# All feature norms of a two-block network: sums by token, root and reciprocal on 128x4, squares in the tail of the adding stages, high part first in the first two units

## What is computed

```python
def rms_norm(x, g):
    xf = x.astype(jnp.float32)
    y = xf * lax.rsqrt(jnp.mean(xf * xf, axis=-1, keepdims=True) + EPS)
    return (y * g.astype(jnp.float32)).astype(x.dtype)

x = x + merged @ w_out[i]
x = x + expert_choice_moe(rms_norm(x, g_moe[i]), w_router[i], w_exp_gate[i], w_exp_up[i], w_exp_down[i])
ple_gate = jax.nn.sigmoid(rms_norm(x, g_ple[i]) @ w_ple_gate[i])
x = x + ple_gate * (p[i] @ w_ple[i])
```

## Time and profile before

| what | value |
|---|---|
| time, median of 3 runs | 4469.36 us (4468.59 to 4471.97) |
| the profiled execution | 4467.54 us, its span 4465.8 us |
| granted PE clock, mean over the span | 0.912 of full speed |
| PE busy | 85% of the span |
| DVE, ACT, POOL busy | 40%, 28%, 3% |

### The profile page before, as it was taken

How to read it: one execution, slowest core, us unless ns; L and a number is a source line. 1 busy time by engine, 2 the same in 40 slices (tenths; PEclk the granted TensorE clock), 3 DMA queues, 4 the chain that set the end, 5 groups by cost and what they waited for, 6 DMA issues and landing times. The chain is left out here.

```text
span 4465.8 us, 46290 instructions
## 1 busy us (share of the span) xinstructions
PE 3794.0 (85%) x17300; PEld 2476.6 (55%) x17300; DVE 1780.6 (40%) x2668; ACT 1269.7 (28%) x1955; POOL 139.8 (3%) x60
## 2 busy tenths in 40 slices
PE   6769999978899979366996999988757798699997
PEld 4557877855688857224875433346523587433334
DVE  5745434177444341756334111133367443311114
ACT  3434433147343221244322000023134332100003
POOL 3500000021000000000000000000000000000000
PEclk8989999989999989667997999999867799799999
DMA  2122222110222321000223899942100121499991
GB/s 113 59 72 83 99 90 81 50 48 16 79 99 80 105 80 48 23 17 18 94 69 123 342 418 410 410 197 71 38 0 17 54 99 54 189 420 412 409 397 47
DMA packets 108849, 617.62 MB, mean 138 GB/s; under 512 B 12310, under 2 KB 12694, under 8 KB 58812
## 3 DMA queue, kind: packets, MB, share of 16 engines
q1 hardware_dynamic: 108732, 616.07, 35.6%
HBM read 612.07 MB, written 3.95 MB: 138 GB/s over the span
## 5 line engine op out<-in xcount | busy, mean ns | idle before, releaser
L325 PE MATMUL PS<-WK_r,RING_r 128*128 128x512 f32 x2096 | 832.2, 397 | 0.0
L323 PE MATMUL PS<-WK_r 128*128 128x512 f32 x1712 | 687.9, 402 | 120.5 <-DVE RING_r L320 67.9
L325 PEld LDWEIGHTS PS<-WK_r,RING_r 128*128 128x128 f32 x2096 | 404.2, 193 | 86.7
L323 PEld LDWEIGHTS PS<-WK_r 128*128 128x128 f32 x1712 | 329.7, 193 | 219.7 <-DVE RING_r L320 78.6
L324 PE MATMUL PS<-HT_r,WK_r 128*128 128x512 f32 (+1 forms) x992 | 395.5, 399 | 0.0
L1944 DVE TENSOR_TENSOR XT<-XT,PS 128x512 f32<-128x512 f32 x128 | 88.0, 687 | 579.2 <-PE PS L1870 579.2
L320 DVE TENSOR_TENSOR RING_r<-RING,WK_r 128x1024 fp32r<-128x1024 f32 x194 | 236.7, 1220 | 73.8 <-ACT WK_r L317 73.8
L325 PE MATMUL PS<-AR_r,RING_r 128*128 128x512 f32 x672 | 263.0, 391 | 0.0
L323 PE MATMUL PS<-AR_r,RING_r 128*128 128x512 f32 x640 | 251.1, 392 | 10.3 <-DVE HT_r L320 10.3
L324 PE MATMUL PS<-AR_r,WK_r 128*128 (+1 forms) x592 | 235.5, 398 | 0.0
L320 DVE TENSOR_TENSOR RING_r<-RING,RING_r 128x1280 fp32r<-128x1280 f32 (+1 forms) x80 | 115.1, 1439 | 291.7 <-ACT RING_r L317 291.7
(11 more groups left out here) (345 smaller groups left out, 5494.2 us busy)
## 6 DMA issues: line engine op xcount, KB each, us to landing
AR<-moe SPq DMA_DIRECT2D x288, 1024.0 KB, 11.1
RING<-moe SPq DMA_DIRECT2D x96, 1024.0 KB, 11.6
RING<-ff_in SPq DMA_DIRECT2D x96, 512.0 KB, 3.4
RING<-branch SPq DMA_DIRECT2D x64, 640.0 KB, 3.8
RING<-ff_out SPq DMA_DIRECT2D x48, 512.0 KB, 3.4
RING<-mix_in SPq DMA_DIRECT2D x32, 512.0 KB, 3.4
RING<-lru_in SPq DMA_DIRECT2D x20, 640.0 KB, 4.8
RING<-ple SPq DMA_DIRECT2D x16, 640.0 KB, 11.5
```

Of the source, the lines that this page charges most:

```text
L323: nc.tensor.matmul(out, r(w_high), r(x_high), start=start, stop=False)
L325: return nc.tensor.matmul(out, r(w_low), r(x_high), start=False, stop=stop)
```

## The change

`norm_pe` no longer sums with ones as the stationary operand. In `token_sums` the squares are stationary, 128 tokens at a time, and one column of ones moves: 4 float32 matmuls of one column for each of 8 pieces, 32 in all, which leave the sums by token on the partitions, 128x4. ACT takes the root of mean plus EPS of these straight from PSUM, DVE the reciprocal of 128x4. To spread the result over the partitions again, DVE multiplies it into an identity matrix (four diagonals, 128x512), and PE multiplies that by ones into bank 6 (`spread`), from where the normed pieces are made.

With `early=True` (the six norms behind an `out_stage`) the squares and the sums are made in the tail of the `out_stage`, before the barrier. `norm_dve` now writes all 8 normed pieces, then the low part of weight unit 1, then all low parts of the pieces. `first_units` takes units 0 and 1 with the high parts of x first and the low parts of x last; it serves the two feed-forward stages, NSA, both mix stages and both embeddings. LRU keeps its order on PE.

```diff
+    def token_sums(b, k, square):
+
+        for t in range(TT):
+            mm = nc.tensor.matmul(bank(b, t, 1), square[:, t * P:(t + 1) * P], cst("ones", 0, 1),
+                                  start=(k == 0 and t == 0), stop=(k == KD - 1), skip_group_check=True)
+        return mm
...
+    def norm_act(act, s, while_summed=None, early=False):
+        if not early:
+            for k in range(KD):
+                nc.scalar.activation(wk(k), XT[:, k], ACT.Square).then_inc(s["squared"], 1)
         if while_summed:
             while_summed()
-        act.wait_ge(s["mean"], 1)
-        nc.scalar.activation(wk(9), wk(8), ACT.Sqrt).then_inc(s["deviation"], 1)
-
-    def norm_pe(pe, s):
+        if not early:
+            act.wait_ge(s["summed"], 1)
+        nc.scalar.activation(STD, bank(0 if early else 7, 0, TT), ACT.Sqrt, bias=cst("eps"), scale=1.0 / D
+                             ).then_inc(s["deviation"], 1)
+
+    def norm_pe(pe, s, early=False):
+        if not early:
+            for k in range(KD):
+                pe.wait_ge(s["squared"], k + 1)
+                mm = token_sums(7, k, wk(k))
+            mm.then_inc(s["summed"], 1)
+        pe.wait_ge(s["diagonal"], 1)
+        nc.tensor.matmul(bank(6), cst("ones"), wk(8), start=True, stop=True).then_inc(s["spread"], 1)
+
+    def norm_dve(dve, s, gain, at=0, out=HT, highs=None, lows=None, first=None, second=None):
+
+        dve.wait_ge(s["deviation"], 1)
+        nc.vector.reciprocal(INV, STD).then_inc(s["inverse"], 1)
+        dve.wait_ge(s["inverse"], 1)
+        nc.vector.tensor_tensor(wk(8).rearrange("p (t c) -> p t c", t=TT), cst("ident").unsqueeze(1).to_broadcast([P, TT, P]),
+                                INV.unsqueeze(2).to_broadcast([P, TT, P]), ALU.mult).then_inc(s["diagonal"], 1)
+        if first:
+            first()
+        dve.wait_ge(s["spread"], 1)
         for k in range(KD):
-            pe.wait_ge(s["squared"], k + 1)
-            mm = nc.tensor.matmul(bank(7), cst("ones"), wk(k), start=(k == 0), stop=(k == KD - 1))
-        mm.then_inc(s["summed"], 1)
-
-    def norm_dve(dve, s, gain, at=0, out=HT, highs=None, lows=None, while_root=None):
-
-        dve.wait_ge(s["summed"], 1)
-        nc.vector.tensor_scalar(wk(8), bank(7), 1.0 / D, EPS, ALU.mult, ALU.add).then_inc(s["mean"], 1)
-        if while_root:
-            while_root()
-        dve.wait_ge(s["deviation"], 1)
-        nc.vector.reciprocal(wk(9), wk(9)).then_inc(s["inverse"], 1)
-        dve.wait_ge(s["inverse"], 1)
-        for k in range(KD):
-            nc.vector.scalar_tensor_tensor(out=out[:, k], in0=XT[:, k], scalar=par(gain, at + k), in1=wk(9),
+            nc.vector.scalar_tensor_tensor(out=out[:, k], in0=XT[:, k], scalar=par(gain, at + k), in1=bank(6),
                                            op0=ALU.mult, op1=ALU.mult).then_inc(s["normed"], 1)
-            if highs and k:
-                dve.wait_ge(s["x_high"], k)
-                low_part(lows[k - 1], HT[:, k - 1], highs[k - 1]).then_inc(s["x_low"], 1)
+        if second:
+            second()
         if highs:
-            dve.wait_ge(s["x_high"], KD)
-            low_part(lows[KD - 1], HT[:, KD - 1], highs[KD - 1]).then_inc(s["x_low"], 1)
+            for k in range(KD):
+                dve.wait_ge(s["x_high"], k + 1)
+                low_part(lows[k], HT[:, k], highs[k]).then_inc(s["x_low"], 1)
 
+    def first_units(pe, s, w, high, banks, highs, lows):
+
+        for u in range(2):
+            pe.wait_ge(s["w_split"], u + 1)
+            for k in range(KD):
+                if u == 0:
+                    pe.wait_ge(s["x_high"], k + 1)
+                at = slice(k * P, (k + 1) * P)
+                nc.tensor.matmul(bank(banks[u]), r(high[u][:, at]), r(highs[k]), start=(k == 0), stop=False)
+                nc.tensor.matmul(bank(banks[u]), r(slot(w, u)[:, at]), r(highs[k]), start=False, stop=False)
+        done = []
+        for u in range(2):
+            for k in range(KD):
+                if u == 0:
+                    pe.wait_ge(s["x_low"], k + 1)
+                at = slice(k * P, (k + 1) * P)
+                mm = nc.tensor.matmul(bank(banks[u]), r(high[u][:, at]), r(lows[k]), start=False, stop=(k == KD - 1))
+            done.append(mm)
+        return done
...
                 unit_loop(pe, unit)
+                for m in range(KD):
+                    pe.wait_ge(s["squared"], m + 1)
+                    mm = token_sums(0, m, SQ[m])
+                mm.then_inc(s["summed"], 1)
...
+                for m in range(KD):
+                    act.wait_ge(s["added"], m + 1)
+                    nc.scalar.activation(SQ[m], XT[:, m], ACT.Square).then_inc(s["squared"], 1)
...
-                norm_pe(pe, s)
-                with pe.Fori(0, FF_N // 2) as i:
+                norm_pe(pe, s, early=True)
+
+                def pair(i, j):
+                    n = i * 2 + j
+                    pe.wait_ge(s["w_split"], 2 * n + 1)
+                    pe.wait_ge(s["b_free"], n + 1)
+                    in_unit(w, 2 * j, j, WH, list(zip(XH, XL))).then_inc(s["used"], 1)
+                    pe.wait_ge(s["w_split"], 2 * n + 2)
+                    in_unit(w, 2 * j + 1, 2 + j, WH, list(zip(XH, XL))).then_inc(s["used"], 1)
...
+                for mm in first_units(pe, s, w, WH, (0, 2), XH, XL):
+                    mm.then_inc(s["used"], 1)
+                pair(0, 1)
+                with pe.Fori(1, FF_N // 2) as i:
                     for j in range(2):
-                        n = i * 2 + j
-                        pe.wait_ge(s["w_split"], 2 * n + 1)
-                        pe.wait_ge(s["b_free"], n + 1)
-                        in_unit(w, 2 * j, j, WH, list(zip(XH, XL)), 0,
-                                None if j else lambda k: pe.wait_ge(s["x_low"], k + 1)).then_inc(s["used"], 1)
-                        pe.wait_ge(s["w_split"], 2 * n + 2)
-                        in_unit(w, 2 * j + 1, 2 + j, WH, list(zip(XH, XL))).then_inc(s["used"], 1)
+                        pair(i, j)
...
                 norm_pe(pe, s)
-                with pe.Fori(0, KD // 4) as i:
-                    for j in range(4):
-                        n = i * 4 + j
+                first_units(pe, s, w, WH, (0, 1), XH, XL)
+                pe.wait_ge(s["p_low"], 2)
+                for n in range(KD):
+                    j = n % 4
+                    if n >= 2:
                         pe.wait_ge(s["w_split"], n + 1)
                         pe.wait_ge(s["free"], n + 1)
-                        in_unit(w, j, j, WH, list(zip(XH, XL)), 0,
-                                None if j else lambda k: pe.wait_ge(s["x_low"], k + 1))
-                        pe.wait_ge(s["p_low"], 2)
-                        in_unit(w, j, 4 + j, WH, list(zip(PH, PL)), KD).then_inc(s["gates_in"], 1)
+                        in_unit(w, j, j, WH, list(zip(XH, XL)))
+                    in_unit(w, j, 4 + j, WH, list(zip(PH, PL)), KD).then_inc(s["gates_in"], 1)
 
             @block.scalar
             def _(act):
@@ -2005,8 +2070,8 @@
...
-                mm = nc.tensor.matmul(bank(b)[0:4], par("rel_bias", 0, 4)[0:BUCKETS], HOT[:, b], start=True, stop=True)
+                mm = nc.tensor.matmul(bank(1 + b)[0:4], par("rel_bias", 0, 4)[0:BUCKETS], HOT[:, b], start=True, stop=True)
             mm.then_inc(s["rows"], 1)
-            norm_pe(pe, s)
+            norm_pe(pe, s, early=True)
             pe.wait_ge(s["shifted"], 16)
             pe.wait_ge(s["copied"], 1)
             for n in range(8):
-                if n >= 7:
-                    pe.wait_ge(s["out_copied"], n - 6)
-                nc.tensor.matmul(bank(n % 7, 0, HALF), cst("flip"), ar(7, 7)[:, n * HALF:(n + 1) * HALF],
+                if n >= 6:
+                    pe.wait_ge(s["out_copied"], n - 5)
+                nc.tensor.matmul(bank(n % 6, 0, HALF), cst("flip"), ar(7, 7)[:, n * HALF:(n + 1) * HALF],
                                  start=True, stop=True).then_inc(s["flipped"], 1)
 
         @block.scalar
         def _(act):
-            norm_act(act, s)
```

More of the change, by code:

```diff
@@ L77, in const_tables @@
         "ones": np.ones((P, P)),
+        "eps": np.full((P, 1), EPS),
         "ones64": (p // 64 == np.arange(P)[None, :] // 64).astype(float),
@@ L263, in arrived @@
         pe.wait_ge(filled[w.first + j], w.before[j] + 16 * (i + 1))
-    NORM = " squared summed mean deviation inverse normed"
+    NORM = " squared summed deviation inverse diagonal spread normed"
     SPLIT = " x_high x_low w_high w_split"
+    STD, INV = SM[:, 456:460], SM[:, 460:464]
     def split_act(act, s, highs):
@@ L375, in out_stage @@
         XH = [wk(4 + b) for b in range(2)]
-        with stage("used highs lows banked added") as (block, s):
+        SQ = [wk(8 + m) for m in range(KD)]
+        with stage("used highs lows banked added squared summed") as (block, s):
             @block.sync
@@ L817, in _, with unit @@
         def _(pe):
-            norm_pe(pe, s)
-            with pe.Fori(0, 4) as i:
```

(31 more changed lines are left out.)

39 lines of the change are left out of this document (20 added, 19 removed).

## The result

The changed kernel takes 4497.61 us (median of 4 runs, 4495.89 to 4503.85) against 4470.66 us of before (4 runs on the same chip): ratio 1.0062, 95% interval 1.0045 to 1.0080. It is slower by 27 us. The prediction was 4490, from 4472 to 4504. The profiled execution took 4496.11 us with a span of 4494.3, 28.5 more than before.

The account below looks back on a forecast made before the run. PE, busy 85% of the span, was taken to bound the kernel, with each norm a gap in its work. The stage terms sum to +20.9 us, 4490.3 on the median of 4469.36; 8-in-10 range 4472 to 4504.

Parts of the forecast that it names:

- the clock stays up: Rival: weight loads count as work, so the new sums run at full clock; 4431 us, faster by 0.8%; chance 0.08.
- it falls late: Rival: the clock falls 5.9 us after the last wide matmul everywhere; 4473 us; chance 0.13 with all milder mixtures.
- the order costs: Rival: under high-first order PE waits longer for unit 2 everywhere, taking back 10 us; 4500 us; chance 0.14.
- The record's price and the clock: Each norm's 64 one-column records: 0.106 us each at full clock, 0.211 at half; 6.8 or 13.5 us, plus 0.3.
- When it falls: During the norm's sums, PE's clock falls to half 4.1 us after the last wide matmul; ends 2.4 and 5.9.
- The tail: Root, reciprocal, diagonals and spread, from the sums' end to the first normed piece: 3.4 us, gaining 1.7, 1.4 and 2.0.
- The LRU: Its late norm's sums start at half clock and never rise: 13.8 us for 9.81, +4.0 - 1.4 = +2.6.
- T: The start of a norm's first normed piece; in the first feed-forward before the change 342.05, 13.27 us behind the last add.
- Routers: Early norms with no weight split but the table load: 13.8 us from last add against 12.9, +1.0 each.
- Embeddings: Longer norm sums +2.4 each, unit 2 starting earlier by the high-first order -2.7 each; together -0.6.
- Between the blocks: Early norm: barrier 8.8 us later behind the last add, bias table's stage 2.6 shorter; net +6.2, between +2 and +8.
- The order: High parts first: unit 2 starts 1.6 us earlier in NSA and mixes, 2.7 in embeddings, 0.2 later in feed-forwards; LRU 0.

Follow-up runs that it names:

- 128 columns: The changed kernel, but each of the 32 sum matmuls moves 128 columns of ones instead of one: 4441.17 us, ratio 0.9935.
- order alone: The kernel before with only the high-part-first order, its norm unchanged: 4465.33 us, ratio 0.9996.
- norm alone: The changed kernel with the old order of normed pieces, low pieces and units: 4505.97 us, ratio 1.0084.
- rounded kernels: The changed kernel with 128 columns of ones, squares and ones in the rounded format: 4419.59 us; the same with the order of before: 4428.06 us.

## Why the prediction was right

The theory was that the sums by token cost more than those that they replace because the clock falls during records of one column. Its rivals were that the clock stays up, that it falls late, and that the order costs. By its steps:

**The record's price and the clock: right.** 0.106 and 0.211 were read from other matmuls; the sums gave 0.112 from start to start and, where PE ran at half clock throughout (the first mix), 13.81 for 64 records (13.5 and the 0.3 of hand-over forecast). The LRU's take the same 13.81 at the same 0.213, though the profile's clock reads 1.00 there, so at the start of the span it is the spacing of the records that tells. The 0.106 was a small misreading: 54 is a window's count, and the gate's records too start 0.112 apart, so 64 at full clock are 7.2 and not 6.8 (7.30 with 128 columns). The kernel with 128 columns turned the loss of 27 us into a gain of 26 by its medians, 29 by its ratio, where the rival of the clock that stays up had 38. That rival had the price of a full clock roughly right; with one column the clock fell. The Trainium skill, "TensorE: Matmul & The Clock Gate", section "HAM oscillation", asks for no long idle gaps; the windows above have none between 328 and 332, and the clock fell there. For records of one column the trace does not bear that rule out.

**When it falls: too late by a little.** I took 4.1 us after the last wide matmul. In the first feed-forward it was 2.3 (327.52 to 329.84), in the ten norms that start at full clock 2.3 to 4.9, 3.6 in the mean; the scatter is as wide as the error. The early norms' sums took 9.2 to 11.6, 10.4 in the mean, where 9.7 was forecast with 0.3 of hand-over; all twelve together 140.9, where the prediction's terms add to 134.6 with their hand-overs. The earlier fall and the price of 0.112 are each about half of it. The milder rival, a late fall, went the wrong way.

**The tail: right.** 3.37 for 3.4; spread 2.08 for 2.1, diagonals 0.69.

**The shifts by stage**, read as after less before at the last adds and first squares, in us:

| stage | forecast | measured |
|---|---|---|
| LRU | +2.6 | -0.3 |
| feed-forwards | +0.5, +1.8 | +1.4, +2.2 |
| NSA | 0.0 | +0.6 |
| between the blocks | +6.2 | +5.0 |
| mixes | +1.5, +2.5 | +0.9, +7.0 |
| routers with experts | +1.0, +1.0 | +3.1, +1.9 |
| embeddings | -0.3, -0.3 | +1.2, +1.2 |
| final norm | +4.4 | +4.4 |

They add to +28.6 where +20.9 was forecast, inside the range but a third more, and the mis-sized terms are these. *The sums* fell short by some 6. *The LRU*: its T came 2.6 later (35.02), as forecast, and its last add did not; two executions of that same code end the block 5 us apart, so -0.3 says nothing against the term. *The second mix*: its norm gave +4.2 (forecast +4.1); what follows its T lasted 748.4 here, and 744.2 to 746.4 in the seven experiments with the same order, so about 3 of its +7.0 belong to this execution. It is luck that these 3 and the LRU's -2.9 cancel in the sum. *Routers*: the first one's sums took 10.94, and T came 15.0 behind the last add for 13.8; behind T the two stages were 1.0 and 1.5 longer than before, which the forecast had at nothing and whose cause stays open. *Embeddings*: the norms cost 3.2 each for 2.4, and the order gave 2.0 back instead of 2.7.

**Between the blocks: the sum right, the reading of it incomplete.** +8.8 for the late barrier and -2.6 for a shorter stage were measured as +8.8 and -3.9. But the term is not the price of being early: with one column, late costs as much. It is the price of long sums in either place. With 128 columns it turns into one, of 4.1 us.

**The order: direction right, size open.** PE's waits ahead of unit 2 came as forecast: NSA 1.08 (1.3), feed-forward 2.90 (3), unit 2 at T + 15.4 (15.6) and T + 18.0 (17.4):

```profile
361.74 0.50 PE L339 MATMUL PS<-WK_r 128*128 128x512 f32 x1 [2.90 <-DVE RING_r L336]
```

```profile
780.58 0.50 PE L339 MATMUL PS<-WK_r,AR_r 128*128 128x512 f32 x1 [1.08 <-DVE RING_r L336]
```

The forecast has it at -9. Each kernel set against before on its own chip, three pairs give -2 (order alone against before), -12 (changed against norm alone) and -3 (rounded kernels). No pair shows a cost, which was the rival of the high-first order. In the traces the stretches from T to the next last add, the LRU's left out, are 6.1, 4.3 and 1.2 shorter in these pairs. The two embeddings have 4.5, 3.9 and 4.6 of that, for 5.4 forecast, and these alone are shown. The 1.6 each of NSA and the mixes is not: those stages came out from 2.7 shorter to 2.6 longer, since a saving of 1.6 in a stage of 745 is less than what that stage varies. The feed-forwards lost 0.2 to 1.3 for the forecast 0.2.

## What to carry to other kernels

Turning a reduction by ones round, so that the data are the stationary operand and one column moves, saves columns and not time: in float32 it was 64 loads of 0.112 us each where 16 wide records had taken 7.1, and with one column the clock fell. If the small result behind it is wanted, try more columns of ones and read the granted clock beside them (51 to 56 us here for two changed lines), and then halve the loads (22 more us, with rounded squares). The wide sums of before with rounded squares, which would be 8 records instead of 16, were not tried, so it is not shown that turning the reduction round is the better way at all. An operation that has been brought forward still stands on the path in its full length when nothing but it is left between the last add and the root.

## What the runs showed of the hardware

At full clock 64 loads with their matmuls took the same with 1 column as with 128 (0.112 us from one record's start to the next), and the granted clock was 0.50 from 330 us on with the first and 1.00 up to 336 with the second, PE being busy without a gap in both. So a PE row that is full does not mean that the clock is held.

VectorE's 128x10 operations took 2.25 to 2.31 us, instead of 0.17, when they started within a GpSimd operation on 128x1024, and ended with it; it was so with two inputs and with one. The Trainium skill, "SBUF — State Buffer", section "SBUF: two separate sides", describes a port pair that one of the two engines holds for a whole instruction while the other waits. The trace agrees for these rows: 46.72 + 2.39 is 49.11, and the short operation ends at 49.14.
